# A fifth block-product step in mixer A's projection, with its tables, sums and waits rearranged

## The chip, the cores and the metric

The kernel runs on one core of a Trainium2 chip. The metric is device time in microseconds (us), from launch to the end of the last instruction; lower is better. Engines: TensorE (PE) multiplies, VectorE (DVE) and ScalarE (ACT) do elementwise work, GpSimd (POOL) does the sums of weight blocks and the rotary step, SyncE (SP) issues nearly all transfers. Each engine works through its own list in order and waits on semaphores.

## The reference, cut to what matters

Two layers, 512 tokens, width 2048, float32:

```
h = rmsnorm(x, norm_g)
aq, ak, av, ag, bq, bk, bv, bg = split(h @ w_in)      # 8 column groups
ya = chunk_relbias_attention(aq, ak, av, rel_bias) * silu(ag)
yb = swa_sink_gqa(rope(bq), rope(bk), bv, sinks)   * silu(bg)
x  = x + concat(ya, yb) @ w_out
```

and one more RMSNorm at the end. Mixer A has 16 heads, in 8 pairs of two heads (128 columns); each pair needs four column tiles of `w_in` (queries, keys, gate, values). With 512 tokens its band covers everything that is causal by chunks.

## The kernel before

**Precision.** Every float32 matrix product is made of three passes over split numbers: weight high part times activation high part, weight high times activation low, weight low times activation high. ACT makes each high part (a copy that rounds) and DVE the low part (the difference).

**Points.** The program goes by points. A point of the projection is one chunk of weights (a quarter of a column tile's 2048 rows, or the equivalent). At a point PE first does what attention wants of it, then its chunk. ACT makes the chunk's high part three points ahead (`hi_in`) and DVE its low part two points ahead (`lo_in`); between those they do the attention steps of the point. The order within a point is written out by hand on each engine, and it is this order that decides who waits.

**Mixer A.** For each pair of heads there are 16 points, called a unit. In unit u PE projects pair u (`unit_sums`, u from 1 to 7), while attention is done for pair u-1. Pair 0 is projected at the start of the layer, with the norm's sums beside it; the attention of pair 7 runs beside the first four tiles of mixer B, in `unit`. Column tiles are projected two at a time, in 8 chunks, each of two k tiles (256 rows) by two column tiles. A plain chunk ("p") is 12 matmuls of 512 columns. A chunk by block products ("s") treats the two by two blocks as Winograd's form of Strassen's scheme does: 7 products of blocks in place of 8, each of three passes, so 21 matmuls of 256 columns. It needs sums of the activations' blocks (`sum_h` on POOL, then `hi_h_sums` on ACT and `lo_h_sums` on DVE, once a layer, at points 8 to 15 before unit 1), sums of the weights' blocks (`sum_w_in` on POOL, four subtractions or additions of 128x128 in each "s" chunk), 7 blocks instead of 4 in the high and low parts (896 columns instead of 512), and after the last "s" chunk the combination of the products (`copy_p1`, `sum_of_products_in`), which `take_pair` adds to the other half and scales.

**Which chunks are what** is set by `IN_CHUNKS`: before, p p s s s s p p, with `IN_SUM_K = 4`. The banks change roles from one pair of tiles to the next, so the first "s" chunk writes where the last pair's sums stood: PE waits for `rows_added` (two additions in `take_pair`) ahead of it, before at the third chunk.

**Attention in a unit.** Eight steps e, four for each head. At points 0, 1, 3, 4, 6, 7, 9, 10 PE makes scores (L765 to L768), DVE adds the bias and takes the row's maximum (`bias_a`, L1630 and L1634), ACT the exponential (L1164), DVE the reciprocal (`invert`, L1655), and ACT at the next point the scaled row. Two points after the scores PE turns the row (`turn_a`, L776), ACT takes its high part (`hi_p`) and DVE its low part (`lo_p`, the `arena<-ps_t,arena` rows of L1562). All steps share one PSUM bank, so turn e waits for `lo_p` of e-1 (`pt_done`): the turn at point 3 waits for the low part made at point 2.

```
            def turn_a(e0, e):
                pe.wait_ge(normed, e0 + (e + 1))
                if e >= 1:
                    pe.wait_ge(pt_done, e0 + e)
```

**`lo_q`, `lo_k`, `gated`.** At points 12 to 15 DVE also makes the low parts of the next pair's queries and keys, combines the products and adds and gates the attention's output in a row of `xy` that SP stores to memory.

**Lines.** DVE's helper `low` is L1562 (all low parts by subtraction) and L1563 (scaled ones), ACT's `copy` is L1099. L881 to L883 are the block products, L894 to L896 the plain ones of `unit_sums`, L719 to L721 those of all other projections. L936 is the mean square of the norm, L1028 the matmul that spreads its root, L2005 and L2008 the two last additions ahead of it (`presum_squares`).

## Time and profile before

| what | value |
|---|---|
| median of 3 runs | 1622.51 us (1622.07 to 1624.85) |
| the profiled execution, its own time | 1622.79 us |
| its span, first to last instruction | 1620.2 us |
| mean granted TensorE clock | 0.994 |
| PE, DVE, ACT, POOL busy | 99%, 77%, 58%, 26% |

The profile names lines of kernel.py. A row of the timeline has the start, the duration, the engine, the line, the operation, what it writes and reads, its shape, a count, and in brackets how long the engine sat idle before it and what ended that. A row of the windows has, after the stretch, the busy time and (in brackets) the number of instructions of PE, PE's weight loads, DVE, ACT and POOL, then the clock, the share of the transfers and GB/s. PE's busy time overlaps itself, since matmuls are pipelined; so a chunk's price is read from start to start. Layer 0 is 0 to about 800 us; its units 1 to 7 run from about 60 to 408 us and its `unit` from 408 to about 457 us. Layer 1 repeats it 797 us later or so.

### The profile page before, as it was taken

The page shows a single profiled execution, that of the slowest core. Times are in us where ns is not written, and L with a number is a line of the kernel's source. Part 1 is how long each engine was busy: PE and PEld are TensorE (multiplying, and loading weights), DVE is VectorE, ACT ScalarE, POOL GpSimd, SP SyncE. Part 2 cuts the span into 40 slices and gives each one's busy share as a digit, 9 for nine tenths or more (in the row PEclk, how much of TensorE's full clock was granted, in tenths as well). Part 3 has the DMA queues.
Part 4 walks back from the last instruction along what each step waited for, and adds up shares of the span by engine and source line. Part 5 has one row for each costly group of instructions (what it writes and reads, how often), then busy time and mean ns, then how long its engine had stood idle before and what let it go on. Part 6 is the DMA issues. An engine that isn't in the chain of part 4 may idle for free.

```text
span 1620.2 us, 28427 instructions
## 1 busy us (share of the span) xinstructions
PE 1595.9 (99%) x9289; PEld 1409.6 (87%) x9289; DVE 1244.2 (77%) x2619; ACT 932.0 (58%) x1969; POOL 420.6 (26%) x554
## 2 busy tenths in 40 slices
PE   9999999999999999999999999999999999999997
PEld 7889989989788888899988998999987888888997
DVE  7787777787567777888877778777775777888874
ACT  7666656656456666433466666666655566664333
POOL 1544353342122210000144335345312321000000
PEclk9999999999999999999999999999999999999998
DMA  6233323333422232344432333333342323223443
GB/s 234 85 103 97 103 90 103 103 103 109 141 94 92 91 111 92 98 156 156 164 117 79 104 104 102 96 94 106 103 155 92 98 94 111 83 91 118 131 143 117
DMA packets 77510, 180.68 MB, mean 112 GB/s; under 512 B 9408, under 2 KB 13792, under 8 KB 70640
## 3 DMA queue, kind: packets, MB, share of 16 engines
q1 hardware_dynamic: 76960, 178.99, 34.0%
q8 instruction: 43, 0.70, 0.2%
q10 hardware_dynamic: 432, 0.55, 0.1%
q14 instruction: 43, 0.35, 0.1%
q0 software_dynamic: 32, 0.08, 0.0%
HBM read 163.25 MB, written 11.62 MB: 108 GB/s over the span
## 4 chain that ended last, share of the span: by engine, by line
PE 90%; DVE 4%; issue 2%; ACT 2%; POOL 1%; DMA 1%; DVEq 0%; SPq 0%; POOLq 0%; ACTq 0%
PE ps_proj L719 9%; PE ps_proj L721 9%; PE ps_proj L720 9%; PE ps_proj L895 3%; PE ps_proj L894 3%; PE ps_proj L896 3%; PE ps_proj L881 3%; PE ps_proj L883 3%; PE ps_proj L882 3%; PE ps_o L789 2%; PE ps_t L776 2%; PE ps_s L881 2%; PE ps_s L883 2%; PE ps_s L882 2%; PE ps_s L894 2%
## 5 line engine op out<-in xcount | busy, mean ns | idle before, releaser
L1562 DVE TENSOR_TENSOR w_lo<-w_raw,w_hi 128x512 fp32r<-128x512 f32 (+1 forms) x528 | 446.4, 853 | 96.5 <-ACT w_hi L1099 91.9
L1099 ACT ACTIVATE w_hi<-w_raw 128x512 fp32r<-128x512 f32 (+1 forms) x528 | 377.9, 725 | 190.9 <-DVE w_raw L1931 66.0
L719 PE MATMUL ps_proj<-act_hi,w_hi 128*128 128x512 f32 x704 | 277.7, 394 | 0.0
L720 PE MATMUL ps_proj<-act_lo,w_hi 128*128 128x512 f32 x704 | 275.4, 391 | 0.0
L721 PE MATMUL ps_proj<-act_hi,w_lo 128*128 128x512 f32 x704 | 275.1, 391 | 0.0
L2258 POOL TENSOR_TENSOR w_raw<-w_raw 128x128 f32<-128x128 f32 x112 | 73.8, 659 | 363.7 <-DMA w_raw<-w 363.7
L1164 ACT ACTIVATE probs<-probs,nmax 128x128 f32<-128x128 f32 (+3 forms) x128 | 72.1, 564 | 148.6 <-DVE nmax L1634 148.6
L721 PEld LDWEIGHTS ps_proj<-act_hi,w_lo 128*128 128x128 f32 x704 | 132.6, 188 | 28.7
L1099 ACT ACTIVATE arena<-ps_t 128x512 fp32r<-128x512 f32 (+4 forms) x168 | 74.8, 450 | 138.7 <-PE ps_t L776 88.0
L719 PEld LDWEIGHTS ps_proj<-act_hi,w_hi 128*128 128x128 f32 x704 | 132.7, 189 | 24.7
L720 PEld LDWEIGHTS ps_proj<-act_lo,w_hi 128*128 128x128 f32 x704 | 132.8, 189 | 24.4
L1562 DVE TENSOR_TENSOR arena<-ps_t,arena 128x512 fp32r<-128x512 f32 (+4 forms) x168 | 84.6, 507 | 41.8 <-ACT arena L1099 41.6
L2223 POOL TENSOR_TENSOR temp<-temp 128x512 f32<-128x512 f32 x13 | 25.0, 1922 | 262.5 <-ACT temp L1234 262.5
L894 PE MATMUL ps_proj<-act_hi,w_hi 128*128 128x512 f32 x224 | 87.8, 392 | 0.4 <-DVE w_lo L1562 0.4
L895 PE MATMUL ps_proj<-act_lo,w_hi 128*128 128x512 f32 x224 | 87.8, 392 | 0.0
L2263 POOL TENSOR_TENSOR w_raw<-w_raw 128x128 f32<-128x128 f32 x112 | 85.4, 763 | 8.8
L896 PE MATMUL ps_proj<-act_hi,w_lo 128*128 128x512 f32 x224 | 87.3, 390 | 0.0
L2230 POOL TENSOR_TENSOR temp<-temp,strips_tables 128x512 f32<-128x512 f32 x18 | 24.4, 1358 | 220.7 <-DVE temp L1574 220.6
L1099 ACT ACTIVATE probs<-probs,rden 128x128 f32<-128x128 f32 (+3 forms) x128 | 70.6, 552 | 15.2 <-DVE rden L1655 15.1
L2261 POOL TENSOR_TENSOR w_raw<-w_raw 128x128 f32<-128x128 f32 x112 | 74.9, 669 | 0.0
L1183 ACT ACTIVATE probs<-probs,nmax 128x128 f32<-128x128 f32 (+1 forms) x128 | 49.0, 384 | 40.7 <-DVE nmax L1648 40.7
L776 PE MATMUL ps_t<-flip_sb,probs 128*128 128x128 f32 x320 | 56.6, 275 | 9.1 <-DVE arena L1562 7.4
(376 smaller groups left out, 4482.9 us busy)
## 6 DMA issues: line engine op xcount, KB each, us to landing
w_raw<-w SPq DMA_DIRECT2D x322, 256.0 KB, 3.0
w_raw<-w SPq DMA_DIRECT2D x51, 1024.0 KB, 4.9
temp<-temp SPq DMA_DIRECT2D x72, 64.0 KB, 4.1
strips_tables<-ext SPq DMA_DIRECT2D x16, 256.0 KB, 4.2
temp<-xT SPq DMA_DIRECT2D x16, 256.0 KB, 4.4
xs<-xy SPq DMA_DIRECT2D x16, 256.0 KB, 4.4
temp<-xs SPq DMA_DIRECT2D x16, 256.0 KB, 4.1
strips_tables<-ext SPq DMA_DIRECT2D x16, 224.0 KB, 4.5
```

Of the source, the lines that this page charges most:

```text
L719: pe.matmul(dst, wh, act_hi[:, k, :], start=start, stop=False)
L720: pe.matmul(dst, wh, act_lo[:, k, :], start=False, stop=False)
L721: return pe.matmul(dst, wl, act_hi[:, k, :], start=False, stop=stop)
L776: mm = pe.transpose(ps_t[0][:, kt * P:(kt + 1) * P], probs[:, e % 2, kt * P:(kt + 1) * P], flip_sb[:, :])
L881: pe.matmul(dst, wh, hi, start=first, stop=False, skip_group_check=True)
L882: pe.matmul(dst, wh, lo, start=False, stop=False, skip_group_check=True)
L894: pe.matmul(dst, hi_f[:, cols], act_hi[:, row, :], start=j == 0 and k == 0, stop=False, skip_group_check=True)
L895: pe.matmul(dst, hi_f[:, cols], act_lo[:, row, :], start=False, stop=False, skip_group_check=True)
L896: mm = pe.matmul(dst, lo_f[:, cols], act_hi[:, row, :], start=False, stop=last, skip_group_check=True)
L1099: return nc.scalar.activation(dst, src, ACT.Copy, scale=scale)
L1562: return nc.vector.tensor_tensor(dst, src, hi, ALU.subtract)
L2263: nc.gpsimd.tensor_tensor(b[S4], b[W12], b[S2], ALU.subtract).then_inc(in_wsum, 1)
```

## The change

1. `IN_SUM_K` goes from 4 to 5 and `IN_CHUNKS` to p s s s s s p p. In each of 28 pairs of tiles (14 in a layer) one plain chunk, the second, becomes a block chunk. PE's wait for `rows_added` moves from the third chunk to the second.
2. The fifth pair of activation tiles (n = 4) needs sums too. They are the first in the new order `H_ORDER`; DVE makes them itself (`sum_last_h`, four subtractions of 128x256), ACT and DVE then make two more high and low parts. `hi_h_sums` waits for the low parts of the pair before it from the second pair on (before: from the third).
3. Their space comes from `y_sum_last`, which shares memory with the rotary tables, from `v_st`, and from the tile `t_ot`. So the tables are loaded in each layer after the last chunk of mixer A (`tables_in`), and the half of the attention's output that ACT copies goes straight into its row of `xy` (`half_out`) instead of `t_ot`; the wait for the store of that row moves from DVE's point 12 to ACT's point 8.
4. `presum_squares` stands one point earlier (9 instead of 10) on DVE.
5. `take_pair` is cut in two. The additions that PE waits for stand at the front of points 0 and 8, ahead of that point's bias; the scaling (`scale_pair`) stays behind.
6. In `unit`, DVE makes each low part of the weights one point later than before: at a point it now takes the chunk whose high part ACT made at the point before.

Cut to its core:

```diff
-IN_SUM_K = 4
-IN_CHUNKS = (("p", 0), ("p", 1), ("s", 0), ("s", 1), ("s", 2), ("s", 3), ("p", 2), ("p", 3))
+IN_SUM_K = 5
+IN_CHUNKS = (("p", 0), ("s", 0), ("s", 1), ("s", 2), ("s", 3), ("s", 4), ("p", 1), ("p", 2))
+H_ORDER = (4, 0, 1, 2, 3)
+H_SUMS_AT = (10, 11, 12, 14, 15)
...
@@ sync @@
+                sp.wait_ge(proj_done, T + A_SLOTS)
+                carry_wait(sp)
+                for dst, src in ((cos_sb, cos), (sin_sb, sin)):
+                    sp.dma_start(dst[:, :], src).then_inc(tables_in, 16)
                 sp.wait_ge(proj_done, T + (A_SLOTS + 1))
...
@@ tensor, unit_sums @@
-                    if i == 2:
+                    if i == 1:
                         pe.wait_ge(rows_added, q * 2 + (2 * L + 2))
...
@@ scalar @@
-                copy(t_ot[64 * h:64 * h + 64, :], ps_o[0][64 - 64 * h:128 - 64 * h, :]).then_inc(o_half, 1)
+                copy(xy[64 * h:64 * h + 64, tile, :], ps_o[0][64 - 64 * h:128 - 64 * h, :]).then_inc(o_half, 1)
...
+            def hi_h_sums(L, m):
+                if m == 0:
+                    act.wait_ge(last_summed, (L + 1) * 4)
+                else:
+                    act.wait_ge(h_summed, (L * (IN_SUM_K - 1) + m) * 4)
+                    act.wait_ge(h_sum_lo, (L * IN_SUM_K + m) * 2)
...
+                    if p == HALF_OUT_AT[0]:
+                        act.wait_ge(h_sum_lo, (L + 1) * (2 * IN_SUM_K))
+                        act.wait_ge(y_kept, L * (16 * (PAIRS - 2)) + u * 16)
...
@@ vector, unit_sums @@
-                    if p == SUM_HALVES_AT[0]:
-                        dve.wait_ge(y_kept, L * (16 * (PAIRS - 2)) + u * 16)
-                        carry_wait(dve)
+                    if p == 0 and not first:
+                        take_pair(T - 4, L, u - 1, 1, GATES_VALUES)
+                    if p == 8:
+                        take_pair(T, L, u, 0, QUERIES_KEYS)
                     attend(att, p, L, ab, Y_STAGE, other)
                     if p == 0 and not first:
-                        take_pair(T - 4, L, u - 1, 1, ((t_graw, 0.5), (t_v, 1.0)))
+                        scale_pair(L, u - 1, 1, GATES_VALUES)
+                    if p == 8:
+                        scale_pair(L, u, 0, QUERIES_KEYS)
...
-                    if p == 8:
-                        take_pair(T, L, u, 0, ((t_q, 1.0), (t_k, 1.0)))
...
+            def sum_last_h(L):
+                n = H_ORDER[0]
+                dve.wait_ge(h_scaled, L * (2 * IN_SUM_K) + 2)
+                y11, y12 = left_right(xy[:, 2 * n, :])
+                y21, y22 = left_right(xy[:, 2 * n + 1, :])
+                nc.vector.tensor_tensor(y11, y12, y11, ALU.subtract).then_inc(last_summed, 1)
...
@@ vector, unit @@
-                for c in range(LO_AHEAD, PTS):
+                for c in range(LO_AHEAD, PTS - 1):
                     lo_next(T, c)
...
-                        attend(att, p, L, ab, ab, lambda: split_w(T, s + 1, pt))
+                        def other():
+                            if p == 0:
+                                lo_next(T, PTS - 1)
+                            else:
+                                split_w(T, (p - 1) // PTS + 1, (p - 1) % PTS)
...
@@ vector, start of the layer @@
-                        if p == 2 * PTS + 2:
+                        if p == 2 * PTS + 1:
                             presum_squares(L)
...
+                        if p == 9:
+                            sum_last_h(L)
```

**DVE at the start of a layer**, from the last high-part wait of point 8 to the reciprocal of the norm's root (L2034 before, L2084 after). Before:

```order
L2005 TENSOR_TENSOR temp<-temp 128x512 [waits acc_done1,acc_done0]
L2008 TENSOR_TENSOR temp<-temp 128x512 [waits presum,sq_done]
L1562 TENSOR_TENSOR w_lo<-w_raw,w_hi 128x512 [waits w_hi_done]
L1562 TENSOR_TENSOR h_sum_t<-xy,h_sum_t 128x512 [waits h_sum_hi] x2
L2034 RECIPROCAL r_cols<-r_cols 128x4 [waits sqrt_done]
```

And with the change:

```order
L2055 TENSOR_TENSOR temp<-temp 128x512 [waits acc_done1,acc_done0]
L2058 TENSOR_TENSOR temp<-temp 128x512 [waits presum,sq_done]
L1578 TENSOR_TENSOR w_lo<-w_raw,w_hi 128x512 [waits w_hi_done]
L1875 TENSOR_TENSOR xy<-xy 128x256 [waits h_scaled]
L1877 TENSOR_TENSOR xy<-xy 128x256 [waits last_summed]
L1879 TENSOR_TENSOR xy<-xy 128x256 [waits last_summed]
L1881 TENSOR_TENSOR xy<-xy 128x256 [waits last_summed]
L1578 TENSOR_TENSOR w_lo<-w_raw,w_hi 128x512 [waits w_hi_done]
L1578 TENSOR_TENSOR temp_r<-xy,y_sum_last 128x512 [waits h_sum_hi,presum]
L1578 TENSOR_TENSOR v_st<-xy,y_sum_last 128x512 [waits h_sum_hi]
L2084 RECIPROCAL r_cols<-r_cols 128x4 [waits sqrt_done]
```

The last two additions of the squares now stand a chunk's low part earlier; between them and the reciprocal there are two low parts of weights instead of one, and the four new subtractions.

**DVE at point 0 of units 2 to 7**, the start of the loop's body (L1809 and L1828 are the waits for the last pair's products). Before:

```order
L1630 TENSOR_TENSOR probs<-ps_s,strips_tables 128x128 [waits s_done]
L1634 ISA probs,nmax<-ps_s,probs 128x128 [waits low_biased]
L1562 TENSOR_TENSOR w_lo<-w_raw,w_hi 128x896 [waits w_hi_done]
L1655 RECIPROCAL rden<-psum_e 128x1 [waits exp_done]
L1809 ISA [waits proj_done]
L1812 TENSOR_TENSOR temp<-ps_s,temp 128x512 [waits in_summed]
L1812 TENSOR_TENSOR temp<-ps_t,temp 128x512
```

And with the change:

```order
L1828 ISA [waits proj_done]
L1831 TENSOR_TENSOR temp<-ps_s,temp 128x512 [waits in_summed]
L1831 TENSOR_TENSOR temp<-ps_t,temp 128x512
L1646 TENSOR_TENSOR probs<-ps_s,strips_tables 128x128 [waits s_done]
L1650 ISA probs,nmax<-ps_s,probs 128x128 [waits low_biased]
L1578 TENSOR_TENSOR w_lo<-w_raw,w_hi 128x896 [waits w_hi_done]
L1671 RECIPROCAL rden<-psum_e 128x1 [waits exp_done]
```

The two additions moved ahead of the bias; nothing was added here.

## Rows read from the trace of the kernel before

**Rows 1.** the page, busy time of the engines
```profile
PE 1595.9 (99%) x9289; PEld 1409.6 (87%) x9289; DVE 1244.2 (77%) x2619; ACT 932.0 (58%) x1969; POOL 420.6 (26%) x554
```

**Rows 2.** PE's waits: for whom, us in total, times, longest
```profile
PE ps_t L776 <- DVE arena L1562: 7.4, 6, 2.3
PE ps_s L936 <- DVE temp L2008: 3.0, 1, 3.0
```

**Rows 3.** windows: from the turn at point 12 to the turn at point 3
```profile
148.30:168.97 20.67, 20.67 (x129) 18.58 (x128) 17.80 (x32) 12.66 (x23) 10.82 (x16) 1.00 0.38 120
```

**Rows 4.** timeline of PE: a plain chunk to what follows, a block chunk likewise
```profile
90.00 0.39 PE L894 MATMUL ps_s<-act_hi,w_hi 128*128 128x512 f32 x1
...
92.76 0.39 PE L767 MATMUL ps_o<-k_st,arena 128*128 128x512 f32 x1
...
93.21 0.28 PE L881 MATMUL ps_s<-act_hi,w_hi 128*128 128x256 f32 x1
...
95.72 0.49 PE L776 MATMUL ps_t<-flip_sb,probs 128*128 128x128 f32 x3
```

**Rows 5.** PE's timeline: turns at point 12 (unit 3), point 3 (unit 4)
```profile
197.84 0.60 PE L776 MATMUL ps_t<-flip_sb,probs 128*128 128x128 f32 x4
...
218.51 0.38 PE L776 MATMUL ps_t<-flip_sb,probs 128*128 128x128 f32 x2
```

**Rows 6.** timeline of DVE between those turns
```profile
200.41 1.39 DVE L1563 SCALAR_TENSOR_TENSOR arena<-temp,arena 64x512 fp32r<-64x512 f32 x2
...
207.93 0.75 DVE L1562 TENSOR_TENSOR w_lo<-w_raw,w_hi 128x512 fp32r<-128x512 f32 x1
...
210.48 0.29 DVE L1630 TENSOR_TENSOR probs<-ps_s,strips_tables 128x128 f32<-128x128 f32 x1 [0.34 <-PE ps_s L765]
...
216.94 1.09 DVE L1562 TENSOR_TENSOR w_lo<-w_raw,w_hi 128x896 fp32r<-128x896 f32 x1 [0.43 <-ACT w_hi L1099]
217.95 0.28 DVE L1562 TENSOR_TENSOR arena<-ps_t,arena 128x128 fp32r<-128x128 f32 x1
```

**Rows 7.** DVE's timeline: low parts of weights elsewhere, POOL idle or at work
```profile
35.93 0.68 DVE L1562 TENSOR_TENSOR w_lo<-w_raw,w_hi 128x512 fp32r<-128x512 f32 x1
38.62 1.22 DVE L1562 TENSOR_TENSOR w_lo<-w_raw,w_hi 128x512 fp32r<-128x512 f32 x1 [2.00 <-ACT w_hi L1099]
...
112.07 1.31 DVE L1562 TENSOR_TENSOR w_lo<-w_raw,w_hi 128x896 fp32r<-128x896 f32 x1
```

**Rows 8.** timeline of DVE and PE at point 3 of unit 2
```profile
118.97 0.28 DVE L1562 TENSOR_TENSOR arena<-ps_t,arena 128x128 fp32r<-128x128 f32 x1
...
119.40 0.41 PE L776 MATMUL ps_t<-flip_sb,probs 128*128 128x128 f32 x2
```

**Rows 9.** PE's timeline in `unit` of layer 0
```profile
419.58 0.41 PE L776 MATMUL ps_t<-flip_sb,probs 128*128 128x128 f32 x2 [2.34 <-DVE arena L1562]
```

**Rows 10.** timeline of DVE ahead of the turn at 419.58
```profile
418.54 0.69 DVE L1562 TENSOR_TENSOR w_lo<-w_raw,w_hi 128x512 fp32r<-128x512 f32 x1 [1.26 <-ACT w_hi L1099]
419.15 0.28 DVE L1562 TENSOR_TENSOR arena<-ps_t,arena 128x128 fp32r<-128x128 f32 x1
```

**Rows 11.** window right after the turn at 419.58
```profile
420.20:423.82 3.62, 3.62 (x11) 2.83 (x10) 1.66 (x5) 2.19 (x6) 0.00 (x0) 0.54 0.00 0
```

**Rows 12.** PE's and DVE's timeline at the start of the layers
```profile
42.17 1.86 PE L936 MATMUL ps_s<-ones_sb,temp 128*128 128x1 f32 x8 [3.00 <-DVE temp L2008]
...
55.70 3.30 DVE L1562 TENSOR_TENSOR k_st<-temp,k_st 64x512 fp32r<-64x512 f32 x4 [1.59 <-ACT k_st L1099]
...
64.22 0.29 DVE L1630 TENSOR_TENSOR probs<-ps_s,strips_tables 128x128 f32<-128x128 f32 x1 [0.18 <-DVE nsink L2103]
...
861.00 0.29 DVE L1630 TENSOR_TENSOR probs<-ps_s,strips_tables 128x128 f32<-128x128 f32 x1 [0.32 <-DVE strips_tables L2106]
```

**Rows 13.** groups of DVE's instructions, shapes apart; busy us, mean ns of one
```profile
L1562 DVE TENSOR_TENSOR h_sum_t<-xy,h_sum_t 128x512 fp32r<-128x512 f32 x12 | 12.2, 1059 | 0.0
...
L1911 DVE TENSOR_TENSOR xy<-xy 128x256 f32<-128x256 f32 x10 | 4.3, 426 | 0.3
```

More of the change, by code:

```diff
@@ L232, in trunk @@
         h_summed = sem("h_summed")
+        last_summed = sem("last_summed")
         h_sum_hi = sem("h_sum_hi")
@@ L1812, in take_pair, with scale_pair @@
                     nc.vector.tensor_tensor(dst, bank_of[:, :], row, ALU.add).then_inc(rows_added, 1)
-                for n, (bank_of, row, (dst, scale)) in enumerate(rows):
+            def scale_pair(L, u, pair, dsts):
+                q = pair_in(L, u, pair * 8)
+                for n, (dst, scale) in enumerate(dsts):
                     dve.wait_ge(rows_added, q * 2 + (2 * L + n + 3))
```

101 lines of the change are left out of this document (58 added, 43 removed).

## The prediction

> **What bounds the kernel now.** First the page: PE is busy 99% of the span, DVE 77%, POOL 26% [rows 1]. So time can only be won on PE's own list, and PE's waits say what is left beside it: 7.4 us at the turns L776, where DVE's low part of the turned row comes late, and 3.0 us at the norm's mean square [rows 2]. A share of 77% hides a stretch in which DVE is as full as PE: from the turn at point 12 to the turn at point 3 of the next unit DVE is busy 17.80 of 20.67 us [rows 3]. That stretch begins and ends with something that PE and DVE hand each other, so I read it instruction by instruction [rows 5, 6]. DVE's low part ends at 218.23 (217.95 and 0.28) and PE turns at 218.51, 0.28 us later; in unit 2 it is 119.25 and 119.40, 0.15 us apart [rows 8], and 0.15 is also what lies between them at a real stall (419.43 and 419.58 [rows 9, 10]). So 0.15 is the hand-over itself, the usual unit has a slack of 0.13 us at this turn, and unit 2 has none. PE bounds the kernel, and DVE is right behind it once in each unit.
>
> **The change, part by part.**
>
> *The chunk.* A plain chunk takes PE 2.76 us (90.00 to 92.76), a block chunk 2.51 (93.21 to 95.72) [rows 4]: 0.25 us less, in 28 pairs, -7.0 us. The Trainium skill (TensorE: Matmul & The Clock Gate, Back-to-back issue gap) gives an isolated matmul N/2.4 + 2.5 ns, an estimate of 2.59 and 2.29 us for the chunks, 0.30 apart; by it this term would be -8.5. The rows of this kernel decide.
>
> *DVE and the turn at point 3.* The new block chunk is the second, so its low part of 896 columns stands at point 15, inside the full stretch. One of 512 takes 0.75 there; one of 896 takes 1.09 with POOL idle and 1.31 beside its sums [rows 6, 7]: +0.35 to +0.55, I take 0.45. POOL's fifth sum falls at points 12 to 13, beside `lo_q`, whose pair takes 1.39 now [rows 6]; at the ratio 1.31/1.09 that is +0.25. Together +0.70. On the other side DVE idles 0.34 us at point 0 until PE's scores come (the bracket at 210.48 [rows 6]), and with the additions of `take_pair` in front there is work for it: -0.34. The low part of point 2 then comes 0.36 later. PE's stretch has one block chunk more and comes 0.25 earlier. The wait is 0.36 + 0.25 - 0.13 = 0.48 us at each of the 12 crossings (into units 2 to 7, two layers): +5.8 us, less 0.3 that unit 2 and one more like it wait already. Bounds: nothing on `lo_q` and 0.35 on the low part gives 0.35 - 0.34 + 0.25 - 0.13 = 0.13 a crossing, +1.6; the upper bound is the ratio of [rows 7], 1.22/0.68 = 1.8 beside POOL's wider sums: 1.09 x 1.8 - 0.75 = 1.2 and 1.39 x 0.8 = 1.1, a wait of 2.3 - 0.34 + 0.12 = 2.1, +25. I take a value near the lower end, because POOL's weight sums are 128x128 and the 1.31 is measured beside just these. Averaged over the units, then, the new chunk and its price cancel but for the other chunk of the unit, and the gain must come from elsewhere.
>
> *The wait for `rows_added`, one chunk earlier.* The additions begin when the last chunk is done and DVE is free, take about 1.3 us (two at 0.68, [rows 7]'s size) and are needed a plain chunk and the scores later, 2.9 us. Hidden; if DVE came 1.3 us later still, it would be the next wait.
>
> *`unit`.* PE's turn at 419.58 waits 2.34 us for DVE, which at 418.54 had waited 1.26 us for a high part that ACT makes in the same point, and only then made the low part at 419.15 [rows 9, 10]. With the shift by one point, the low part of the weights is one whose high part is long there. The same pattern makes all six waits, 7.4 us [rows 2]. After the one in layer 0 the granted clock is 0.54 and 9 matmuls (the row counts two more that began before it) take 3.6 us, at 0.23 each 2.1 [rows 11]: 1.5 more. -7.4 - 1.5 = -8.9 us. Bounds: -9, all of it, and -4, if ACT's scaled row is late next instead. I take all of it; about 1 us should be left between low part and turn.
>
> *The start of a layer.* `presum_squares` a point earlier runs in DVE's idle 2.00 us (the bracket at 38.62 [rows 7]), so PE's 3.00 us wait at L936 goes [rows 12]. But the end of this stage is set by DVE: what matters is when it makes the first bias of unit 1 (64.22 and 861.00 [rows 12]), on which PE's second turn hangs. Added before it: four subtractions at 0.43 alone [rows 13], about 0.7 beside POOL and with their waits, 2.9; two low parts of sums at 0.68 to 1.06 each [rows 7, 13], 2.0 at most; 0.4 for the wider chunk. That is 5.3. Taken back in layer 0: about 0.9 of the 2.00, 0.8 because it no longer waits for PE at the spread of the norm, 1.4 of the 1.59 until ACT's `k_st` [rows 12], and 0.7 as the two additions no longer stand beside POOL: 3.8 or a little more, so I take +1.1 us net. In layer 1 PE did not wait at the norm, less idle time can be filled, and ACT's `hi_h_sums` now waits for the low parts before it: +2.0. Sum +3.1. PE's 3.0 us wait thus does not turn into time; it moves to the spread of the norm, where I expect 2 to 4 us, and to the first `rows_added`, which DVE now signals after point 0's chunk is done. Bounds: -1 us a layer if the squares' clock loss goes and POOL hinders less, +3 a layer.
>
> *Edits at nothing.* The tables (two transfers of 256 KB after mixer A's last chunk) are needed at the first rotary step, some 20 us later. ACT's wait for the stored row stands at point 8, the store is issued at points 1 to 2. POOL's 28 sums more are idle time of an engine at 26%. If a table were late, the first rotary step would be, and it has several points' cover.
>
> **The sum.** -7.0 + 5.8 - 0.3 - 8.9 + 3.1 = -7.3 us on the profiled execution's 1622.8 (span 1620.2 and 2.6 around it): **1615.5 us**. The median of the runs, 1622.5, is 0.3 lower, which changes nothing. A measurement of this kernel can tell about 0.2%, 3.2 us, from no change; so "faster" is below 1619.3.
>
> **The rivals.**
>
> *DVE has more room (0.18).* POOL's sum misses `lo_q`, and the start costs 1 us in all: -7.0 + 1.6 - 0.3 - 8.9 + 1.0 = -13.6, 1609 us. For it: the slowdown beside POOL is a fifth only. Against: DVE idles just 2.9 of 20.67 us [rows 3], part of it before the stretch's work can begin.
>
> *The crossings eat it all (0.20).* Where DVE has no idle time to fill, as in unit 2 [rows 8], the wait is 0.70 + 0.25 = 0.95. If all crossings are like that, +11.4, and the start costs 4.5: -7.0 + 11.4 - 0.3 - 8.9 + 4.5 = -0.3, 1622.5, no change.
>
> *The wait in `unit` changes its name (0.12).* -4 in place of -8.9: 1620.4, no change. For it: ACT scales the row in the same points.
>
> *POOL blocks DVE (0.10), slower.* The fifth sum hinders DVE in the full stretch as POOL's wide sums do at 38.62, by 1.8. The wait at a crossing is 2.1, +25: -7.0 + 25 - 0.3 - 8.9 + 3.1 = +11.9, 1634.7. It decides from a wait of 1.35 us a crossing, which with the rest gives +3.2. The Trainium skill (SBUF — State Buffer, Who interferes with whom) says that a DVE instruction with two inputs in SBUF contends with a GpSimd instruction that reads SBUF, and that the later one is blocked outright. That rule speaks against this change, since `lo_q` and the low parts have two such inputs. The 1.22 us at 38.62 [rows 7] agrees with it, the 1.31 at 112.07 [rows 7] shows a small price for POOL's small instructions.
>
> **How the numbers follow.** The forecast has 0.40. Range: 1608.5 (the first rival, a little below) to 1624; above it lie the last rival and a start dearer than my bound, below it a gain at every crossing, together 0.2. Faster: most of the forecast (0.37), the first rival, 0.05 of the others, 0.60. Slower: the last rival and 0.03, 0.13. Same 0.27.
>
> **What would show it.** Right: no waits of L776 in `unit`, a short wait of about 0.5 us at the turn of point 3 in units 2 to 7, units of 49.5 us as before, L936 without a wait but the spread with one, the first bias of unit 1 1 to 2 us later against the start of its layer. Wrong: crossings without waits or with over 1 us, PE waiting for `rows_added` inside the units, a turn in `unit` that waits for ACT's scaled row, a block chunk beyond 2.6 us.

## The result and the profile after

The changed kernel takes 1629.55 us (median of 7 runs, 1629.11 to 1632.3) beside 1623.95 for the kernel before on the same chip: ratio 1.0038, 95% interval 1.0025 to 1.005. It is slower by 0.4%. The ratios here and below leave out two executions far outside the rest, 1740.08 us of the kernel before (1623.33 without it) and 5162.41 us of run 10. Forecast was 1615.5, and 1624 as the upper end of the range. The profiled execution took 1629.48 us with a span of 1627.2 (before 1622.8 and 1620.2), so 7.0 us of span have to be found. Lines of the changed kernel have other numbers: the turns are L786 (L776 before), low parts L1578 and L1579 (L1562, L1563), the additions of `take_pair` L1831, its scaling L1838, the block products L891 to L893 (L881 to L883), ACT's `copy` L1109 (L1099), the spread of the norm's root L1038 (L1028).

The page of the changed kernel, its busy line, answers to [rows 1]:
```profile
PE 1588.8 (98%) x9541; PEld 1416.4 (87%) x9541; DVE 1282.0 (79%) x2631; ACT 945.8 (58%) x1977; POOL 487.9 (30%) x666
```
PE is busy 7.1 us less and waits more. PE's waits (us in total, times, longest), beside [rows 2]:
```profile
PE ps_t L786 <- DVE arena L1578: 14.6, 12, 1.3
PE ps_s L1038 <- DVE r_cols L2084: 5.0, 2, 4.4
PE ps_proj L891 <- DVEq L2150: 4.1, 2, 2.3
PE ps_t L729 <- DVE act_lo L1579: 1.8, 1, 1.8
```
The six waits of the turns in `unit` are gone. In their place stand 12 at other turns, one at each crossing into units 2 to 7 of both layers, 1.2 us each where 0.48 were forecast; 5.0 us at the spread of the norm and 4.1 at the first `rows_added` (L2150) are the starts of the layers. The last of the four lines is a wait at 9.31 us, in the first projection; it is 1.9 us long in run 5 and 0.5 in run 6, which differ in nothing there. Laid along PE's landmarks, the turns, the 7.0 us divide so (working: start of the later landmark less start of the earlier, in each trace):

| stretch on PE | before | after | difference | forecast |
|---|---|---|---|---|
| to the first turn of unit 1, layer 0 | 66.82 | 70.39 | +3.57 | +1.1 |
| to the turn at point 12 of unit 7 | 329.35 | 334.50 | +5.15 | -0.75 |
| to the last turn in `unit` | 57.19 | 50.97 | -6.22 | -8.9 with layer 1 |
| to the mean square of layer 1 | 386.68 | 387.43 | +0.75 | 0 |
| to the first turn of unit 1, layer 1 | 23.45 | 26.90 | +3.45 | +2.0 |
| to the turn at point 12 of unit 7 | 328.94 | 333.98 | +5.04 | -0.75 |
| to the last turn in `unit` | 54.83 | 50.97 | -3.86 | |
| to the end | 372.94 | 372.06 | -0.88 | 0 |

`unit` gave 10.1, the units lost 10.2 where 1.5 should have been won, the two starts cost 7.0 in place of 3.1. Of the error of 14.3 us (7.0 longer instead of 7.3 shorter) 11.7 are in the units, and there they sit at one place; 3.9 are in the starts. Window of the changed kernel from the turn at point 12 of unit 3 to the turn at point 3 of unit 4 (us, then busy time of PE, PEld, DVE, ACT, POOL, clock, DMA share, GB/s), the stretch of [rows 5]:
```profile
202.84:224.69 21.85, 20.60 (x139) 18.88 (x137) 19.49 (x32) 13.00 (x23) 13.74 (x20) 1.00 0.38 112
```
DVE's timeline in that stretch (start, us, engine, line, form, idle time before and releaser), beside [rows 6]:
```profile
205.42 1.56 DVE L1579 SCALAR_TENSOR_TENSOR arena<-temp,arena 64x512 fp32r<-64x512 f32 x2
207.01 0.84 DVE L1578 TENSOR_TENSOR w_lo<-w_raw,w_hi 128x512 fp32r<-128x512 f32 x1
207.77 3.56 DVE L1578 TENSOR_TENSOR k_st<-temp,k_st 64x512 fp32r<-64x512 f32 x4
...
212.13 0.41 DVE L1814 TENSOR_TENSOR temp<-ps_proj,temp 128x256 f32<-128x256 f32 x1
...
213.71 1.28 DVE L1578 TENSOR_TENSOR w_lo<-w_raw,w_hi 128x896 fp32r<-128x896 f32 x1
...
216.54 0.69 DVE L1831 TENSOR_TENSOR temp<-ps_s,temp 128x512 f32<-128x512 f32 x1
...
218.44 1.22 DVE L1578 TENSOR_TENSOR w_lo<-w_raw,w_hi 128x896 fp32r<-128x896 f32 x1
...
219.65 1.74 DVE L1838 SCALAR_TENSOR_TENSOR temp<-temp,rstd 128x512 f32<-128x512 f32 x2
...
223.25 1.09 DVE L1578 TENSOR_TENSOR w_lo<-w_raw,w_hi 128x896 fp32r<-128x896 f32 x1 [0.44 <-ACT w_hi L1109]
224.26 0.28 DVE L1578 TENSOR_TENSOR arena<-ps_t,arena 128x128 fp32r<-128x128 f32 x1
```
POOL's timeline at its start:
```profile
204.94 0.46 POOL L2311 TENSOR_TENSOR w_raw<-w_raw 128x128 f32<-128x128 f32 x1 [9.32 <-DMA w_raw<-w]
205.48 0.95 POOL L2313 TENSOR_TENSOR w_raw<-w_raw 128x128 f32<-128x128 f32 x1
206.39 0.91 POOL L2314 TENSOR_TENSOR w_raw<-w_raw 128x128 f32<-128x128 f32 x1
207.38 0.79 POOL L2316 TENSOR_TENSOR w_raw<-w_raw 128x128 f32<-128x128 f32 x1
```
For comparison, the rows of the kernel before that the forecast did not use, first DVE's, then the first of POOL's:
```profile
201.83 0.69 DVE L1562 TENSOR_TENSOR w_lo<-w_raw,w_hi 128x512 fp32r<-128x512 f32 x1
202.44 3.12 DVE L1562 TENSOR_TENSOR k_st<-temp,k_st 64x512 fp32r<-64x512 f32 x4
...
211.18 1.18 DVE L1562 TENSOR_TENSOR w_lo<-w_raw,w_hi 128x896 fp32r<-128x896 f32 x1
...
213.54 1.54 DVE L1815 SCALAR_TENSOR_TENSOR temp<-temp,rstd 128x512 f32<-128x512 f32 x2
```
```profile
203.17 0.96 POOL L2258 TENSOR_TENSOR w_raw<-w_raw 128x128 f32<-128x128 f32 x1 [13.31 <-DMA w_raw<-w]
```
The low part of the turned row, on which PE's turn hangs, begins 21.42 us after the turn at point 12 (224.26 - 202.84); before it was 20.11 (217.95 - 197.84 [rows 5, 6]). Averaged over the 12 crossings the two are 21.40 and 20.11. I call this number the DVE time of a crossing; it is what the experiments are read by. In the rows `lo_q` takes 1.56, not 1.39; the low part at point 15 1.28, not 0.75; the idle 0.34 us are gone. But the low part of 512 at 207.01 (0.84 for 0.69), `lo_k`'s four (3.56 for 3.12) and the scaling (1.74 for 1.54) are longer too, and the forecast had nothing on these. And the last rows show another thing: the turn itself waits only for 0.28 us of work at 224.26, which stands in DVE's queue behind a low part of weights of 1.09 us, for which DVE had waited 0.44 besides.

**Why DVE's instructions are longer.** The rows themselves say it, if the ends are laid side by side. POOL's sum at 206.39 ends at 207.30, and DVE's low part, begun at 207.01, ends at 207.85, 0.55 us after it. POOL's next sum, begun at 207.38, ends at 208.17, 0.32 us after DVE. Alone the low part takes 0.69 us and the sum 0.46 us: whichever of the two begins later ends its own time less 0.14 us after the other. So each of POOL's sums that falls beside DVE's instructions with both inputs in SBUF costs DVE 0.32 - 0.14, about 0.17 us (0.86 in place of 0.69). Over the whole trace of the changed kernel, 277 instructions of DVE with both inputs in SBUF begin while POOL has more than 0.15 us of an elementwise instruction left; 273 of them end by this rule within 0.02 us (worked out from the trace, with each form's time alone). In the other four it is POOL's instruction that was held up.

### The profile page after: what moved, and what is told of

Its sections match the earlier page's. It is cut to its first block, busy times and chain, and to the rows that moved or that the text cites. A ratio compares the mean times of both kernels' runs of the same rounds, so it can differ in the third digit from the quotient of the medians.

```text
span 1627.2 us, 29380 instructions
## 1 busy us (share of the span) xinstructions
PE 1588.8 (98%) x9541; PEld 1416.4 (87%) x9541; DVE 1282.0 (79%) x2631; ACT 945.8 (58%) x1977; POOL 487.9 (30%) x666
## 4 chain that ended last, share of the span: by engine, by line
PE 75%; DVE 16%; issue 4%; ACT 2%; DMA 1%; DVEq 1%; SPq 0%; ACTq 0%
PE ps_proj L729 10%; PE ps_proj L730 10%; PE ps_proj L731 10%; DVE w_lo L1578 4%; DVE k_st L1578 2%; PE ps_proj L891 2%; PE ps_proj L892 2%; PE ps_proj L893 2%; PE ps_t L786 2%; PE ps_proj L905 2%; PE ps_proj L904 2%; PE ps_proj L906 2%; PE ps_o L799 1%; PE ps_s L893 1%; PE ps_s L891 1%
## 5 line engine op out<-in xcount | busy, mean ns | idle before, releaser
L1578 DVE TENSOR_TENSOR w_lo<-w_raw,w_hi 128x512 fp32r<-128x512 f32 (+1 forms) x528 | 462.8, 885 | 50.0 <-ACT w_hi L1109 45.4
L1109 ACT ACTIVATE w_hi<-w_raw 128x512 fp32r<-128x512 f32 (+1 forms) x528 | 386.8, 742 | 193.0 <-DVE w_raw L1981 57.7
L729 PE MATMUL ps_proj<-act_hi,w_hi 128*128 128x512 f32 x704 | 276.9, 393 | 0.0
L730 PE MATMUL ps_proj<-act_lo,w_hi 128*128 128x512 f32 x704 | 274.8, 390 | 0.0
L731 PE MATMUL ps_proj<-act_hi,w_lo 128*128 128x512 f32 x704 | 274.7, 390 | 0.0
L2311 POOL TENSOR_TENSOR w_raw<-w_raw 128x128 f32<-128x128 f32 x140 | 98.7, 705 | 306.7 <-DMA w_raw<-w 306.6
L1109 ACT ACTIVATE arena<-ps_t 128x512 fp32r<-128x512 f32 (+4 forms) x168 | 75.0, 451 | 134.6 <-PE ps_t L786 84.4
L1578 DVE TENSOR_TENSOR arena<-ps_t,arena 128x512 fp32r<-128x512 f32 (+4 forms) x168 | 84.5, 507 | 45.1 <-ACT arena L1109 44.5
L2313 POOL TENSOR_TENSOR w_raw<-w_raw 128x128 f32<-128x128 f32 x140 | 92.8, 663 | 11.0
L2316 POOL TENSOR_TENSOR w_raw<-w_raw 128x128 f32<-128x128 f32 x140 | 89.7, 641 | 11.0
L2314 POOL TENSOR_TENSOR w_raw<-w_raw 128x128 f32<-128x128 f32 x140 | 83.4, 596 | 0.0
L786 PE MATMUL ps_t<-flip_sb,probs 128*128 128x128 f32 x320 | 56.7, 275 | 15.2 <-DVE arena L1578 14.6
L1109 ACT ACTIVATE probs<-probs,rden 128x128 f32<-128x128 f32 (+3 forms) x128 | 70.6, 551 | 0.6 <-DVE rden L1671 0.5
L891 PE MATMUL ps_proj<-act_hi,w_hi 128*128 128x256 f32 x210 | 62.9, 299 | 4.1 <-DVEq L2150 4.1
L904 PE MATMUL ps_proj<-act_hi,w_hi 128*128 128x512 f32 x168 | 65.8, 392 | 0.5 <-DVE w_lo L1578 0.5
```

The lines of the kernel that those rows point to most:

```text
L729: pe.matmul(dst, wh, act_hi[:, k, :], start=start, stop=False)
L730: pe.matmul(dst, wh, act_lo[:, k, :], start=False, stop=False)
L731: return pe.matmul(dst, wl, act_hi[:, k, :], start=False, stop=stop)
L786: mm = pe.transpose(ps_t[0][:, kt * P:(kt + 1) * P], probs[:, e % 2, kt * P:(kt + 1) * P], flip_sb[:, :])
L891: pe.matmul(dst, wh, hi, start=first, stop=False, skip_group_check=True)
L904: pe.matmul(dst, hi_f[:, cols], act_hi[:, row, :], start=j == 0 and k == 0, stop=False, skip_group_check=True)
```

## The experiments

Each ratio is to the kernel before, run beside the experiment (medians 1623.1 to 1624.2 us). The changed kernel was not run again; what is said against it goes by the 1629.55 us above.

**1. The shift in `unit` alone.** The kernel before with this edit and nothing else:
```diff
-                for c in range(LO_AHEAD, PTS):
+                for c in range(LO_AHEAD, PTS - 1):
                     lo_next(T, c)
...
-                        attend(att, p, L, ab, ab, lambda: split_w(T, s + 1, pt))
+                        def other():
+                            if p == 0:
+                                lo_next(T, PTS - 1)
+                            else:
+                                split_w(T, (p - 1) // PTS + 1, (p - 1) % PTS)
+                        attend(att, p, L, ab, ab, other)
...
+                split_w(T, 4, PTS - 1)
```


> The kernel before with the shift in `unit` alone (low parts of the weights one point later), nothing else. Theory U: the waits at the turns in `unit` and the clock loss behind them belong to this edit alone, and none of the price to it. The changed kernel's trace puts the gain at 6.2 us in layer 0 and 3.9 in layer 1, so 1612.7 against 1622.8, no waits at the turns of `unit`, units of 49.54 us as before. Rival: part of the gain in the changed kernel came from PE being later against DVE when it reached `unit` (waits at the crossings had given DVE time); then the turns in `unit` still wait here and the gain is 4 to 6 us, 1617 to 1619.

Measured 1612.65 us, ratio 0.9941 (0.9925 to 0.9958), span 1610.4: 9.8 less. The stretch right after the second turn of `unit`, window of this kernel, beside [rows 11]:
```profile
417.45:421.00 3.55, 3.55 (x18) 2.99 (x17) 1.57 (x5) 2.56 (x6) 0.00 (x0) 1.00 0.05 21
```
The clock is 1.00 where it was 0.54, and 18 matmuls go where 11 went. Layer 0 gives 6.0, layer 1 3.8. The loss of clock stands in layer 0 alone: in the kernel before, the turn at 1215.84 of layer 1 waits 2.33 us, as long as that of layer 0, and the granted clock of the 2.16 us from it on is 1.00. The edit stands by itself, theory U holds. Run once more beside the later kernels it took 1613.26, ratio 0.9933 (0.992 to 0.9945):

> The shift in `unit` alone once more, to stand beside the run before it on the same chip. 1612 to 1613. If the fifth block product is worth anything once its waits are gone, the run before it is faster by 2 us or more; if the two are within 1 us, the block product has paid for itself and no more.

**2. All edits of order, four block products.** To the kernel of run 1 come `presum_squares` at point 9 and the split of `take_pair`:
```diff
-                        if p == 2 * PTS + 2:
+                        if p == 2 * PTS + 1:
                             presum_squares(L)
...
+                    if p == 0 and not first:
+                        take_pair(T - 4, L, u - 1, 1, GATES_VALUES)
...
                     attend(att, p, L, ab, Y_STAGE, other)
                     if p == 0 and not first:
-                        take_pair(T - 4, L, u - 1, 1, ((t_graw, 0.5), (t_v, 1.0)))
+                        scale_pair(L, u - 1, 1, GATES_VALUES)
```


> The changed kernel's three edits of order (squares one point earlier, the additions of take_pair in front, the shift in `unit`), with four of eight k pairs as block products and tables, buffers and POOL's work as before. Theory A: the whole loss of the changed kernel is the fifth block product (at the crossings and at the start of a layer). Then this kernel has no wait at the turns at point 3, units of 49.5 us or a little less, a start of a layer no dearer than before (-3 to 0 us each) and a time of 1607 to 1613 us. Rival B: the order of take_pair or of the squares costs by itself; then the units are longer than 49.6 us or the first turn of unit 1 comes later than 66.8 us, and the time is above that of the `unit` shift alone.

Measured 1614.76 us, ratio 0.9943 (0.9927 to 0.996). That is above the 1607 to 1613 of theory A and within the noise of run 1; its span is 1.8 us longer (1612.2 beside 1610.4). DVE's timeline in the stretch, in which the turn at point 12 is at 197.21 (L1815 is an addition, L1822 the scaling):
```profile
209.87 0.69 DVE L1815 TENSOR_TENSOR temp<-ps_s,temp 128x512 f32<-128x512 f32 x1
...
211.77 1.24 DVE L1562 TENSOR_TENSOR w_lo<-w_raw,w_hi 128x896 fp32r<-128x896 f32 x1
...
213.00 1.74 DVE L1822 SCALAR_TENSOR_TENSOR temp<-temp,rstd 128x512 f32<-128x512 f32 x2
...
217.62 0.28 DVE L1562 TENSOR_TENSOR arena<-ps_t,arena 128x128 fp32r<-128x128 f32 x1
```
The additions fill the idle time (no bracket at 211.07, where the bias stands), and yet the low part comes at 20.41, later than before (20.11); over the 12 crossings 20.35 beside 20.11. What is filled in goes into a slower low part and scaling (1.24 and 1.74; before 1.18 and 1.54) and `lo_k` (3.29; 3.12). The idle time to be filled was small: in the kernel before DVE idles 0.34 to 0.43 us ahead of point 0's bias in four of the 12 crossings, 0.12 in one and 0.03 to 0.06 in the other seven, 0.16 on average, and here 0.10 is left. And the order costs: the two additions, one input of which is in PSUM, are not held up by POOL; moved away, they leave the first scaling beside POOL's sums (0.88 us on average for 0.68). Units are 49.67 us on average (49.58 in run 1). Where the 1.8 us of span are lost is another place: from the last turn in `unit` to the mean square of layer 1 this kernel takes 388.44 us, run 1 386.68. So both theories are half right: the chunk makes the loss of the changed kernel, and the order of `take_pair` brings nothing at the crossing, but costs 0.24 us of DVE time there.

**3. POOL's fifth sum left out.** Its four instructions are missing; three sums of weights are old values.
```diff
                 pool.wait_ge(in_raw[IN_PLACE[i]], raw_count(L, u, j))
+                if i == 1:
+                    pool.sem_inc(in_wsum, 4)
+                    return
```


> The changed kernel, with POOL's four additions for the new block product (the second chunk of each half) left out: its three sums of weights are then old values, and nothing else changes. Theory C (POOL beside DVE): of the 1.33 us by which DVE's stretch from the turn at point 12 to the turn at point 3 grew, about 1.0 is DVE being slower beside POOL's longer burst (lo_q +0.2, lo_k +0.4, the other low parts and the scaling +0.5), 0.35 is width. Then the wait at the turn of point 3 falls from 1.25 to 0.2 to 0.5 us, units to 49.4 to 49.8 us, and the time by 9 to 13 us, to 1617 to 1621. Rival D (width): the longer low part does it; then the wait stays at 1.0 or more and the time within 3 us of 1629.5.

Measured 1618.05 us, ratio 0.9965 (0.9952 to 0.9977). PE's waits:
```profile
PE ps_t L786 <- DVE arena L1578: 7.4, 12, 0.9
```
and DVE's timeline, turn at point 12 at 200.11:
```profile
202.69 1.39 DVE L1579 SCALAR_TENSOR_TENSOR arena<-temp,arena 64x512 fp32r<-64x512 f32 x2
204.10 0.69 DVE L1578 TENSOR_TENSOR w_lo<-w_raw,w_hi 128x512 fp32r<-128x512 f32 x1
204.72 3.33 DVE L1578 TENSOR_TENSOR k_st<-temp,k_st 64x512 fp32r<-64x512 f32 x4
...
220.98 0.28 DVE L1578 TENSOR_TENSOR arena<-ps_t,arena 128x128 fp32r<-128x128 f32 x1
```
DVE does exactly the same work, and `lo_q`, the low part behind it and `lo_k` take 1.39, 0.69 and 3.33 (before 1.39, 0.69 and 3.12). The DVE time of a crossing is 20.80 on average: 0.60 us of the 1.29 are POOL's four small instructions, close to the 4 x 0.17 that the rows above give. The waits fall by half, the starts by 1.6 and 1.3 us (first turn of unit 1 at 68.79). Theory C holds, weaker than foretold at the crossings (0.6 for 1.0), and the rest of the 10.1 us of span comes from the starts.

**4. The low part of the new chunk made narrow.** Three sums of weights keep old low parts.
```diff
+                cols = slice(in_place(i).start, in_place(i).start + PLAIN) if i == 1 else in_place(i)
-                low(lo_f[:, in_place(i)], raw_f[:, in_place(i)], hi_f[:, in_place(i)].bitcast(F32)).then_inc(w_lo_done, 1)
+                low(lo_f[:, cols], raw_f[:, cols], hi_f[:, cols].bitcast(F32)).then_inc(w_lo_done, 1)
```


> The changed kernel, with the low part of the new block product made for 512 of its 896 columns only (the low parts of three sums of weights are old values). Theory C: width is 0.35 to 0.4 us of a crossing, so the wait falls from 1.25 to about 0.85 us, and the time by 4 to 5 us, to 1625. Rival D (width is nearly all): the wait falls below 0.4 us and the time to 1618 to 1620, level with the run that leaves POOL's sum out.

Measured 1624.53 us, ratio 1.0008 (0.9998 to 1.0017); the wait is 0.85 us (10.1 in all), the DVE time 21.02: width is 0.38 us of a crossing. Against the 20.35 of run 2, POOL's sum (0.60) and the width (0.38) make 21.33, measured 21.40. The crossing is accounted for.

**5. The first turned row moved up.** In the changed kernel, the copies of the turned row of score 0 no longer stand behind a low part of weights:
```diff
# ACT
+                if p == 1:
+                    hi_p(g, e0, 0)
-                if p in TURN_A:
+                elif p in TURN_A[1:]:
                     hi_p(g, e0, TURN_A.index(p))
                 if p in SCORES_A:
                     exp_a(e0, SCORES_A.index(p))
# DVE
                 other()
+                if p == 1:
+                    lo_p(e0, 0)
-                if p in TURN_A:
+                elif p in TURN_A[1:]:
                     lo_p(e0, TURN_A.index(p))
```


> The changed kernel; only the two copies of the first turned row (score 0: ACT's high part, DVE's low part) move up, on ACT ahead of the second row's exp at point 1, on DVE ahead of point 2's low part of weights and of the reciprocal. Theory F: PE's turn at point 3 waits for DVE only because that low part of 0.28 us stands behind a low part of 896 columns (1.09 us) for which DVE waited besides. Moved up, it is done a microsecond earlier, and the turn waits next for ACT's scaled second row, some 0.9 us earlier than now. Wait at the turn 0.3 to 0.5 us in place of 1.25, units 49.6 us, time 1617 to 1620. Rival G: DVE's work as a whole is what is late at the crossing (too much of it, in whatever order); then the low part of weights pushed back is late for its chunk in turn, PE waits there instead, and units stay at 50.3 us or more.

Measured 1618.33 us, ratio 0.9968 (0.9957 to 0.998). PE's timeline at point 3 of unit 3:
```profile
171.77 0.44 PE L786 MATMUL ps_t<-flip_sb,probs 128*128 128x128 f32 x2 [0.20 <-ACT probs L1109]
```
and ACT's ahead of it:
```profile
170.39 0.94 ACT L1109 ACTIVATE w_hi<-w_raw 128x896 fp32r<-128x896 f32 x1
171.23 0.49 ACT L1109 ACTIVATE probs<-probs,rden 128x256 f32<-128x256 f32 x1
```
DVE's 0.28 us now begin 19.81 us after the turn at point 12, and the turn waits for ACT's scaled row (11 waits of at most 0.4 us, 2.6 in all), which in turn stands behind a high part of weights, as theory F said. The low part of weights pushed back is late for nobody inside the units, which take 49.49 us, so rival G falls.

**6. The scaled row ahead of the high part as well.** To run 5 come:
```diff
# ACT
+                        if p == 2:
+                            hi_in(T, L, u, 1 + HI_AHEAD)
...
-                        else:
+                        elif p != 1:
                             hi_in(T, L, u, p + HI_AHEAD)
# DVE: invert ahead of lo_p at point 1
                 if p in SCORES_A:
                     invert(e0, SCORES_A.index(p))
+                if p == 1:
+                    lo_p(e0, 0)
```


> As the run before, and on ACT the scaling of the second row now stands ahead of the high part of point 1's weights, on DVE the reciprocal ahead of the moved low part. Theory F: the turn then comes another 0.3 us earlier, waits of 0 to 0.2 us at point 3, units of 49.2 to 49.4 us, 1613 to 1617 us. Rival G as before; and if ACT's high part, pushed back 0.6 us, holds up DVE and PE's chunk at point 4, units are no shorter than in the run before.

Measured 1616.21 us, ratio 0.9957 (0.9944 to 0.9969), 13 us under the changed kernel. Window of the stretch of unit 3 to 4:
```profile
200.02:220.59 20.57, 20.57 (x138) 18.88 (x137) 18.39 (x31) 11.59 (x22) 14.06 (x20) 1.00 0.34 111
```
PE is busy for all of its 20.57 us, and no turn at point 3 is listed with a wait. POOL is as busy as in the changed kernel. The slowdown of DVE is thus still there; it only stands behind nothing that PE needs. The units take 49.26 us, 0.27 less than the 49.53 of a unit with four block products; two chunks at 0.25 should give 0.50. Of the rest 0.09 is the spacing before the turn at point 3 (0.21 us on average, 0.12 where nothing presses, up to 0.32); what is left is spread over spacings too small to be listed, and its cause stays open.

**7. The control: the same move with four block products** (run 1 and the edit of run 5).

> Control for the moved copies of the first turned row: the kernel before with the shift in `unit` and the same move (without the one of the scaling). With four block products the turn at point 3 has 0.13 us in hand and hardly a wait. Theory F: there is nothing for the move to give back, 0 to 1.5 us, 1611 to 1613. Rival: the move helps by itself, whatever the chunk; then units get shorter than 49.4 us and the time falls by 3 us or more, below 1609.5.

Measured 1612.85 us, ratio 0.9927 (0.9911 to 0.9944), units of 49.53 us. DVE's low part comes 1.4 us earlier (18.71), and PE's stretch stays at 20.67. The move gives back what the chunk took and has nothing of its own, as expected.

**8. The last low parts of sums moved out of the start.**
```diff
-                        if p in H_SUMS_AT:
+                        if p in H_SUMS_AT[:-1]:
                             lo_h_sums(L, H_SUMS_AT.index(p))
+                dve.wait_ge(k_done, L * V_LAYER + 1)
                 take(T, 3, t_v, ps=ps_t[1])
# unit_sums, behind attend
+                    if first and p == 2:
+                        lo_h_sums(L, IN_SUM_K - 1)
```


> The changed kernel with the last two low parts of sums at the start of a layer moved from point 15 to point 2 of unit 1, where DVE waits about 1 us for PE anyway. Theory S (the start of a layer is bound by DVE's list up to the first bias of unit 1, so what is taken off that list comes back in full): the first turn of unit 1 comes 1.4 to 1.7 us earlier in each layer, 2.5 to 3.3 us in all, 1626.5; crossings as in the changed kernel. Rival: the start is bound by PE's waits for ACT or POOL; then nothing changes, 1629.5.

Measured 1626.64 us, ratio 1.0019 (1.001 to 1.0028). The first turn of unit 1 comes at 68.33 in layer 0, 2.06 earlier, and 1.71 earlier against the mean square in layer 1; 3.1 us of span are left of these 3.8. As theory S said.

**9. The four subtractions on DVE left out**; the fifth pair's sums are then the scaled rows.
```diff
-                nc.vector.tensor_tensor(y11, y12, y11, ALU.subtract).then_inc(last_summed, 1)
...
+                dve.sem_inc(last_summed, 4)
```


> The changed kernel without the four subtractions of sum_last_h on DVE (the sums for the fifth k pair are then only the scaled rows). Theory S (the start of a layer is bound by DVE's list): 3.4 to 3.5 us of work leave it, and the first turn of unit 1 comes 2.5 to 3.5 us earlier in each layer, the wait at the spread of the norm falls from 4.4 to 1 to 2 us, time 1622.5 to 1624.5. Rival: DVE's low parts wait for ACT or POOL anyway; then the gain is under 1 us a layer, 1627.5 or more.

Measured 1628.85 us, ratio 1.0031 (1.002 to 1.0042): the expectation failed, and the time is the rival's. The first turn is only 1.64 us earlier in layer 0 and 0.98 in layer 1. DVE's timeline shows why:
```profile
42.75 0.90 DVE L1578 TENSOR_TENSOR w_lo<-w_raw,w_hi 128x512 fp32r<-128x512 f32 x1 [2.58 <-ACT w_hi L1109]
```
Where the subtractions stood, DVE now waits 2.58 us for a high part that ACT makes behind five scaled rows. The first half of the start is bound by ACT, only the second half by DVE's list. Theory S holds for what stands behind that point (run 8), not for what stands before it.

**10. The moved turn and the late low parts together** (runs 6 and 8).

> Both together. If the crossings and the start are two separate prices, the gains add: 1610 to 1614 us, level with or under the kernel before with the shift in `unit` alone (1612.65).

Measured 1611.58 us, ratio 0.9928 (0.9915 to 0.9941): the gains add (18.0 us where 13.3 and 2.9 make 16.2). This and runs 1 and 7 are the best versions, and their intervals overlap; the spans are 1609.4, 1610.4 and 1609.6. With its waits taken away the fifth block product pays for its own start of a layer and for at most 1 to 2 us more (1611.58 beside 1612.65, 1613.26 and 1612.85): the units of both layers take 4.3 us less than those of run 1, the starts 2.9 more.

**11. One sum more moved out.** On top of run 10:
```diff
-                    if first and p == 2:
-                        lo_h_sums(L, IN_SUM_K - 1)
+                    if first and p in (1, 3):
+                        lo_h_sums(L, IN_SUM_K - 2 + p // 3)
...
# ACT, behind attend; unit 1 stands ahead of the loop over units
+                    if first and p == 2:
+                        hi_h_sums(L, IN_SUM_K - 1)
...
```


> The version with the moved turn and the late low parts, and now the low parts of the fourth sum too go from point 14 to point 1 of unit 1, the high and low parts of the fifth to points 2 and 3. Theory S: another 0.7 to 1.7 us a layer, 1608.5 to 1610.5. Rival: unit 1 has no idle time of DVE left for them; then PE waits in unit 1 for a turn or for the sums' low parts, and the time is level with 1611.6 or above.

Measured 1614.48 us, ratio 0.9936 (0.9923 to 0.9949). The first turn comes at 66.58, 1.5 us earlier, and PE then stands at point 4 for the sums' low parts:
```profile
75.54 0.35 PE L891 MATMUL ps_proj<-act_hi,w_hi 128*128 128x256 f32 x1 [2.19 <-DVE h_sum_t L1585]
```
The rival was right in time, 3 us above run 10. Its reason, a DVE without idle time, is not what the rows show. The low parts that PE waits for end at 75.39, and ahead of them, from 71.27 to 74.12, DVE idles three times for ACT, 1.25 us in all, the longest here:
```profile
72.13 1.09 DVE L1585 TENSOR_TENSOR w_lo<-w_raw,w_hi 128x896 fp32r<-128x896 f32 x1 [0.86 <-ACT w_hi L1109]
```
So they are late by their place in DVE's order, behind instructions that wait for ACT; whether another place would do was not tried. Beside the repeat of run 1 (1613.26), which was to tell what the fifth product is worth, this kernel is 1.2 us slower.

## Why the prediction was wrong, step by step

**The chunk: right.** PE's timeline of the changed kernel, from the first matmul of the new block chunk to the turn behind it, beside [rows 4]:
```profile
167.61 0.29 PE L891 MATMUL ps_proj<-act_hi,w_hi 128*128 128x256 f32 x1
...
170.12 0.27 PE L786 MATMUL ps_t<-flip_sb,probs 128*128 128x128 f32 x1
```
It takes 2.51 us, as forecast, for the plain chunk's 2.76. The units without waits (run 6) show only about half of the -7.0 that this gives. The -8.5 worked out from the page "TensorE: Matmul & The Clock Gate" (Back-to-back issue gap) of the Trainium skill is further off.

**DVE and the turn at point 3: the step that failed.** The forecast was +0.70 - 0.34 = +0.36 us of DVE time and a wait of 0.48. Measured are +1.29, and PE's stretch is 21.83 on average, where 20.67 less 0.25 would do: 1.41 us at each of 12 crossings, 16.9 in all instead of the 5.5 of the sum (+5.8 - 0.3). Against the 20.58 that run 6 reaches it is 1.25, 15.0 in all. By its terms:
- "+0.45" for the low part at point 15: right in size, 0.38 (run 4).
- "+0.25" for POOL's fifth sum beside `lo_q`: 0.60 (run 3). `lo_q` itself has +0.17 in the rows and +0.22 on average, as said. The mistake was to look at `lo_q` alone. The new sum is made for a chunk whose weights land one point earlier, so POOL's burst begins 2.10 us after the turn (204.94 - 202.84) and no longer 5.33 (203.17 - 197.84), and DVE's instructions stand under it from there on: the low part at 207.01 has +0.15 and `lo_k` +0.26 on average besides. Each of the four sums costs about 0.17, wherever it falls on such instructions.
- "-0.34" for the additions in front: +0.24 (run 2). The bracket of one unit was taken for all crossings, where the average is 0.16, and the scaling that now stands beside POOL's sums costs more than the idle time that is filled.

**The rival "POOL blocks DVE"** had 0.10. Its mechanism is what happens, and its price is not. The Trainium skill (SBUF — State Buffer, Who interferes with whom) says that a DVE instruction with two inputs in SBUF contends with GpSimd's reads, that one with at most one such input, outside the modes that use both ports, does not, and that the contention is an exclusive lock. This trace agrees with all three: the later of the two is held up until the other's end (207.30 and 207.85, and 273 of 277 instructions), and the sums at 212.13, with one input in PSUM, take 0.41 to 0.43 us in every unit, whether POOL works or not. The 1.31 at 112.07 [rows 7], which the prediction set against this rule as a small price, follows it: in the kernel before, a sum of POOL runs from 111.97 to 112.43, and DVE's 1.09 less 0.14 behind that end at 113.38. What the rival had wrong is the factor of 1.8. It comes from subtractions of 128x256, which hold DVE up for longer; the weight sums of 128x128 cost about 0.17 each, so the DVE time grew by 1.29 and not by 2.0. Its condition, over 1.35 us a crossing, is met by PE's stretch (1.41) and not by the listed wait (1.22). The middle rival, 0.95 a crossing without any idle time to fill, was closer than the forecast; I should have given the two together more than the main case, since the -0.34 rested on the row of a single unit.

**`rows_added` one chunk earlier: right**, no wait inside the units. **Edits at nothing: right**, neither the tables nor the stored row appear among PE's waits, and run 9, which has both edits, takes 386.68 us between the layers, as the kernel before.

**`unit`: right**, -10.1 for -8.9, and run 1 shows that it belongs to this edit. The bound of -9 was too tight: the 7.4 us of listed waits leave out the hand-over of 0.15 us behind each of six, 0.9, which also goes; with the 1.5 of the clock in layer 0 that makes 9.8.

**The start of a layer: mechanism right, size off.** +7.0 for +3.1. PE's 3.0 us wait did move to the spread of the norm and to the first `rows_added`, but as 5.0 and 4.1. DVE's and PE's timeline of the changed kernel, beside [rows 12, 13]:
```profile
40.58 0.96 DVE L1875 TENSOR_TENSOR xy<-xy 128x256 f32<-128x256 f32 x1
...
44.09 1.21 DVE L1578 TENSOR_TENSOR w_lo<-w_raw,w_hi 128x512 fp32r<-128x512 f32 x1
45.22 1.21 DVE L1578 TENSOR_TENSOR temp_r<-xy,y_sum_last 128x512 fp32r<-128x512 f32 x1
46.35 1.21 DVE L1578 TENSOR_TENSOR v_st<-xy,y_sum_last 128x512 fp32r<-128x512 f32 x1
```
```profile
47.70 0.58 PE L1038 MATMUL ps_s<-eye_sb,r_cols 128*128 128x128 f32 x1 [4.40 <-DVE r_cols L2084]
```
The subtractions take 0.82 to 0.96 (0.7 assumed) and the low parts 1.21, above the 0.68 to 1.06 assumed: they follow the same rule, beside POOL's subtractions of 128x256. What the forecast left out altogether is that POOL's fifth sum of weights is in this stretch too: without it, the first turn comes 1.60 us earlier in layer 0 and 1.31 in layer 1 (run 3). The wider low part, 0.4 in the forecast, is 1.38 in layer 0 and 0.36 in layer 1 (run 4); the figures of layer 0 are uncertain by about 0.7, as the four kernels with one and the same start below show. The squares and the order alone save nothing in layer 0 that can be told (first turn at 66.14 in run 2, at 66.21 to 66.95 in the four kernels without them) and 0.4 us in layer 1.

Open stay 0.75 us between the layers, of which 0.4 is one wait of L997 for a low part; runs 2 and 6 have such waits of 0.2 to 0.9 us too (run 2 at the same place, its L987), the kernel before and run 1 have none. Open is also the 0.9 us less at the end; over the runs that stretch is 372.0 to 373.6 us long.

## What to carry to other kernels

A queue that is full between two hand-overs is not slack minus new work: count each instruction of a neighbour that holds yours up, at a price read from the ends of rows, over the whole burst and not beside one instruction. Take idle time from all the repeats of a stretch and not from one row. When such a stretch makes PE wait, first look at what the awaited instruction stands behind: here a copy of 0.28 us stood behind 1.1 us that nobody needed yet. Moving it gave back 11 us (run 5), as much as leaving POOL's sum out (11.5, run 3), and 13 with the scaled row (run 6). And test each edit of a bundle by itself: one of them held all the gain.

## What the hardware showed that I had not expected

DVE and POOL do not slow each other down by some factor; the later one stands still until the earlier one ends, and the longer duration in its row is that standing. It is clearest beside the widest instructions. In the changed kernel, POOL's row and then DVE's:
```profile
577.95 1.29 POOL L2286 TENSOR_TENSOR temp<-temp 128x512 f32<-128x512 f32 x1
```
```profile
577.96 1.82 DVE L1578 TENSOR_TENSOR w_lo<-w_raw,w_hi 128x512 fp32r<-128x512 f32 x1
```
POOL takes what it takes alone and ends at 579.24; DVE ends at 579.78, 0.54 us later. DVE's 128x512 low part from SBUF, 0.69 us alone, takes 0.84 beside sums of 128x128, 1.21 beside subtractions of 128x256 and up to 1.82 here; what tells these apart is how much of POOL's instruction is left when DVE begins, and a wider one has more to leave. DVE's own subtraction of 128x256 takes 0.82 to 0.96 for the 0.43 of [rows 13]. POOL pays by the same rule: its 128x128 takes 0.46 us where DVE reads PSUM, and mostly 0.79 to 1.19 beside DVE's low parts. Groups of DVE's instructions with forms kept apart (busy us, mean ns of one), the changed kernel and then run 3, show what POOL's four sums do to the 72 pieces of `k_st`:
```profile
L1578 DVE TENSOR_TENSOR k_st<-temp,k_st 64x512 fp32r<-64x512 f32 x72 | 59.3, 824 | 1.1 <-ACT k_st L1109 0.3
```
```profile
L1578 DVE TENSOR_TENSOR k_st<-temp,k_st 64x512 fp32r<-64x512 f32 x72 | 56.5, 785 | 1.0 <-ACT k_st L1109 0.3
```
The second thing is small and general: a wait as listed is 0.15 to 0.2 us shorter than the gap on PE that it makes (1.28 listed for the turn at 174.19, for a gap of 1.45), so a term that counts many short waits comes out an eighth too low.
